# RWKV state step and decay product by heads: 64 rows and 64 columns each, in the two halves of a bank's partitions

## The reference

```python
def step(S, inp):
    r_t, w_t, k_t, v_t, a_t, b_t = inp
    sa = jnp.einsum('bhvk,bhk->bhv', S, a_t)
    S = S * w_t[:, :, None, :] + sa[..., None] * b_t[:, :, None, :] + v_t[..., None] * k_t[:, :, None, :]
    return S, jnp.einsum('bhvk,bhk->bhv', S, r_t)
```

## Time and profile before

| | us |
|---|---|
| median of 3 runs | 3189.41 |
| lowest, highest | 3189.28, 3194.16 |
| the profiled execution | 3187.53 |
| its span, first to last instruction | 3185.4 |
| TensorE busy, share of the span | 2967.0, 93% |
| VectorE busy | 2137.2, 67% |
| ScalarE busy | 1572.4, 49% |
| mean granted clock of TensorE | 0.975 |

### The profile page before, as it was taken

How to read it: one execution, slowest core, us unless ns; L and a number is a source line. 1 busy time by engine, 2 the same in 40 slices (tenths; PEclk the granted TensorE clock), 3 DMA queues, 4 the chain that set the end, 5 groups by cost and what they waited for, 6 DMA issues and landing times.

```text
span 3185.4 us, 50274 instructions
## 1 busy us (share of the span) xinstructions
PE 2967.0 (93%) x19942; PEld 2651.2 (83%) x19942; DVE 2137.2 (67%) x3465; ACT 1572.4 (49%) x2606; POOL 714.3 (22%) x885
## 2 busy tenths in 40 slices
PE   4876999999999997899999899888999999999998
PEld 4865998888888887788888788766788888888887
DVE  8787877765777557667766666555756665566655
ACT  3445555543555444455555555344544444344443
POOL 5356402210112000765555410000100111001100
PEclk9987999999999999999999999998999999999999
DMA  4411555556555555322222222422555555555554
GB/s 178 161 67 40 168 176 189 194 171 198 200 186 186 167 166 175 119 79 91 87 87 87 94 90 100 166 80 90 174 181 176 187 194 171 190 211 186 189 170 144
DMA packets 78953, 475.20 MB, mean 149 GB/s; under 512 B 8129, under 2 KB 11201, under 8 KB 37441
## 3 DMA queue, kind: packets, MB, share of 16 engines
q1 hardware_dynamic: 76480, 459.66, 42.5%
q10 hardware_dynamic: 2240, 12.32, 1.1%
HBM read 465.66 MB, written 6.29 MB: 148 GB/s over the span
## 4 chain that ended last, share of the span: by engine, by line
PE 75%; DVE 13%; ACT 7%; issue 2%; POOL 2%; DMA 0%; ACTq 0%; DVEq 0%; SPq 0%; POOLq 0%
PE bank L692 33%; PE bank L696 22%; PE bank L694 5%; PE bank L695 4%; DVE m L1185 3%; ACT m L2006 2%; PE bank L708 1%; DVE m L1839 1%; PE bank L994 1%; POOL m L2679 1%; POOL m L2675 1%; PE bank L995 1%; PE bank L1109 1%; PE bank L991 1%; PE bank L997 1%
## 5 line engine op out<-in xcount | busy, mean ns | idle before, releaser
L696 PE MATMUL bank<-m,m 128*128 128x256 f32 x6864 | 1932.0, 281 | 0.0
L692 PE MATMUL bank<-m,m 128*128 128x512 f32 x4736 | 1656.6, 394 | 2.5 <-ACT m L2497 2.0
L1185 DVE TENSOR_TENSOR m<-m,m 128x1024 fp32r<-128x1024 f32 (+1 forms) x944 | 1076.7, 1149 | 615.0 <-ACT m L2006 609.0
L696 PEld LDWEIGHTS bank<-m,m 128*128 128x128 f32 x6864 | 1302.5, 190 | 1.2
L2006 ACT ACTIVATE m<-m 128x1024 fp32r<-128x1024 f32 (+1 forms) x944 | 911.8, 979 | 724.0 <-PE bank L696 697.4
L692 PEld LDWEIGHTS bank<-m,m 128*128 128x128 f32 x4736 | 890.0, 188 | 200.8 <-issue 2.5
L694 PE MATMUL bank<-m,m 128*128 128x256 f32 x2128 | 643.4, 302 | 74.2 <-DVE m L1185 67.2
L695 PE MATMUL bank<-m,m 128*128 128x256 f32 x2128 | 607.7, 286 | 0.0
L694 PEld LDWEIGHTS bank<-m,m 128*128 128x128 f32 x2128 | 413.6, 194 | 104.5 <-issue 87.8
L695 PEld LDWEIGHTS bank<-m,m 128*128 128x128 f32 x2128 | 414.2, 195 | 3.6 <-issue 1.9
L2656 POOL TENSOR_TENSOR m<-m,m 128x256 fp32r<-128x256 f32 x44 | 63.4, 1441 | 695.6 <-ACT m L2228 695.6
(11 more groups left out here) (368 smaller groups left out, 3057.5 us busy)
## 6 DMA issues: line engine op xcount, KB each, us to landing
m<-in_w_up SPq DMA_DIRECT2D x88, 1024.0 KB, 4.8
m<-in_w_down SPq DMA_DIRECT2D x128, 704.0 KB, 4.0
m<-in_w_gu SPq DMA_DIRECT2D x88, 1024.0 KB, 4.9
m<-in_w_out SPq DMA_DIRECT2D x48, 1024.0 KB, 5.0
m<-in_w_krv SPq DMA_DIRECT2D x48, 1024.0 KB, 4.8
m<-in_w_xbc SPq DMA_DIRECT2D x24, 1024.0 KB, 4.9
m<-in_w_z SPq DMA_DIRECT2D x16, 1024.0 KB, 4.8
m<-in_w_in SPq DMA_DIRECT2D x14, 1024.0 KB, 4.9
```

The lines of the kernel that those rows point to most:

```text
L692: pe.matmul(bank.rearrange("p (a b) -> p a b", a=2), hi, x, start=kc == L.k0, stop=False)
L696: m = pe.matmul(ps, lo, x[:, 0, :], start=False, stop=last)
L1185: v.tensor_tensor(lo_of(k), raw_of(k)[0], hi_of(k).bitcast(F32), SUB).then_inc(*lo_v(("lo", k)))
```

## The change

The decay product becomes two: for each half R of the partitions, the 64 columns R of the weights with the 64 columns R of each of the four chunks (256 columns), written into the partitions R of the bank. Lines 994, 995 and 997 become two each: for each half R, 64 columns of weights with 64 columns, written into rows R and columns R of the bank. In line 997 the old state's columns R still enter with all 128 rows. Line 991, all waits, all signals and what VectorE and ScalarE do are as before; the signal of each group sits on its last matmul. The off-diagonal parts of the bank, which nothing reads, are not computed.

```diff
@@ -977,8 +977,10 @@
                 yield
                 pe.wait_ge(*wkv_a["bkx", i, hf])
                 pe.wait_ge(*wkv_v["q", i, hf])
-                pe.matmul(bB[:, :], wub[:, 128:256], bxb.rearrange("p c k -> p (c k)"), start=True,
-                          stop=True).then_inc(*wkv_pe(("g", i, hf)))
+                for R in HALVES:
+                    m = pe.matmul(bB[R, :].rearrange("p (c k) -> p c k", c=4)[:, :, R], wub[:, 128:256][:, R],
+                                  bxb[:, :, R], start=True, stop=True)
+                m.then_inc(*wkv_pe(("g", i, hf)))
                 yield
                 pe.wait_ge(*wkv_v["g", i, hf])
                 for c in range(4):
@@ -991,10 +993,13 @@
                         m = pe.matmul(bA[:, Q], sb_, qb[:, Q], start=False, stop=c == 3)
                         if c == 3:
                             m.then_inc(*wkv_pe(("y", i, hf)))
-                    pe.matmul(bB[:, 0:128], bxb[:, c, :], wub[:, 0:128], start=True, stop=False)
-                    m = pe.matmul(bB[:, 0:128], kxb[:, c, :], tk[:, TV, :], start=False, stop=first)
+                    for R in HALVES:
+                        pe.matmul(bB[R, R], bxb[:, c, R], wub[:, R], start=True, stop=False)
+                    for R in HALVES:
+                        m = pe.matmul(bB[R, R], kxb[:, c, R], tk[:, TV, R], start=False, stop=first)
                     if not first:
-                        m = pe.matmul(bB[:, 0:128], gb[:, c, :], sb_, start=False, stop=True)
+                        for R in HALVES:
+                            m = pe.matmul(bB[R, R], gb[:, c, R], sb_[:, R], start=False, stop=True)
                     m.then_inc(*wkv_pe(("s", i, hf, c)))
                     yield
```

## The result

| | before | after |
|---|---|---|
| median, us (12 runs each) | 3189.49 | 3183.85 |
| lowest, highest | 3188.92, 3194.16 | 3177.97, 3187.22 |
| profiled execution, us | 3187.53 | 3187.22 |
| its mean granted clock | 0.975 | 0.970 |

The ratio is 0.9979 (95% interval 0.9971 to 0.9988): 5.6 us faster by the medians, where 18 were forecast. The direction was right and the size was three times too large. The same kernel on another chip gave 3183.3 (11 runs, ratio 0.9977).

The account below looks back on a forecast made before the run. TensorE's own stream was taken as the bound in most rounds. State steps and decay products together shorten it by 22.7 us, of which four fifths, 18 us, get through: forecast 3171 us, range 3158 to 3186.

Parts of the forecast that it names:

- The price of a half-width pass: State step and decay product on TensorE: a pair of passes with 64 columns takes 0.055 us, bounds 0.04 and 0.11.
- the overlap of the halves: TensorE's half-width passes: the two halves run side by side, the second pair starting some 0.06 us behind the first.
- the 0.10 us of emptying: At each change of width TensorE empties for 0.10 us; in and out, with the bare loads, 0.365 us.
- the bare loads: Weight loads not hidden at a change of width: 0.055 us into half width, 0.11 us into full width.
- the counts of neighbours: Steps with line 991, by following work: 74 of 112 save 0.055 us each, 30 save 0.42, 8 save 0.265.
- program-order: Rival, 8%: second half waits for the first half's second pass; 8.9 us of stream left, 7 get through, 3182 us.
- no-overlap rivals: Rival, 5%: halves do not overlap at this size, each pair costs 0.11 us; 31 us slower, 3221 us.
- What gets through: Of 22.7 us saved in TensorE's stream, four fifths become time, 18 us; TensorE's waits swallow the rest.
- a rival with 7%: Clock falls, or unseen costs, 7%: clock 0.96 over some 560 us of the stage loses 22 us against 18 gained, 3193.
- The sign that I named for this rival: Trace after: a granted clock below 0.98 from 1400 to 1700 us would show the forecast wrong.
- VectorE takes over after 1760: Rival, 15%: all gain outside 1400 to 1760 us is swallowed, 13 us stay, 3177 us.
- Waits at line 991 grow: TensorE's waits at line 991, for the evacuation of the previous state, grow by some us.

Follow-up runs that it names:

- the second set: The changed kernel, not altered, run once more on another chip beside later runs: 3183.30 us, ratio 0.9977 to the kernel before.
- The full-width run with less work: Kernel before with the decay product streaming 256 of its 512 columns at full width, leaving out chunks 2 and 3: 3190.13 us, ratio 1.0001.
- the filler: Changed kernel plus five unused full-width fp32 products ahead of line 993's wait (line 991 before), even pairs 0 to 10: 3180.17 us; in the kernel before 3189.54.
- before with prep split: Kernel before with VectorE's last five operations of prep split over two rounds: 3192.37 us, ratio 1.0005.
- decay alone: Kernel before with only the decay product by heads, the state step at full width: 3191.98 us, ratio 1.0009.
- 256 columns: Kernel before with the decay product streaming 256 of its 512 columns at full width: 3190.13 us, ratio 1.0001.
- state alone: Changed kernel with the decay product back at full width, only the state step by heads: 3186.65 us, ratio 0.9995 to the kernel before.
- changed with prep split: Changed kernel with VectorE's last five operations of prep split over two rounds: 3182.67 us, ratio 0.9977 to the kernel before.
- line 991 by heads, decay at full width: Changed kernel with line 991 also by heads and the decay product back at full width: 3178.33 us, ratio 0.9962 to the kernel before.
- line 991 by heads: Changed kernel with line 991 also made two half-width products of 64 weight columns and 32 columns: 3171.75 us, ratio 0.9947 to the kernel before.
- the three with the filler: Five spare products in TensorE's wait: changed kernel 3180.17 us, kernel before 3189.54, changed kernel with line 991 also by heads 3173.33.

## Why the prediction was wrong

- **The price of a half-width pass, the overlap of the halves, the 0.10 us of emptying, the bare loads and the counts of neighbours**: right, each within 0.02 us a step, but for 16 of the decay products (0.13 for 0.08); sum 21.5 by kinds of rounds, 22.6 by the balance, for 22.7. The program-order and no-overlap rivals did not come: four passes in 0.11 us.
- **What gets through** is the step that failed. I let four fifths through, for waits alone, 4.5 us of loss, and put the clock's share at nothing. The waits took about what I gave them, 5.6 us in the blocks. The clock took 12.0 us there (14 by the mean clock of the 12 runs, 9 by the second set), and 5.0 us were left of 22.6.
- **The missing term is the clock.** I had it as a rival with 7% and made it hang on the emptied 0.10 us and on a loss over the whole stage. What I held against it, that a stretch with TensorE busy 137 of 145 us holds 1.00, says nothing of what follows a single wait. In its place the runs showed falls behind waits that the shorter stream lengthens: eight slow stretches in the blocks instead of two. Of the six further ones, four follow waits for VectorE (at 1379 behind 1.84 us, 1.66 before; at 1553 and 1706 behind 1.7, 1.35 before; at 1959 behind 1.21, 0.70 before) and two follow waits for ScalarE (at 1792 behind 1.94, 1.89 before; at 1884 behind 1.88, 1.66 before). The full-width run with less work shows that a shorter stream brings it without half width too, the filler that the wait does. Why the one fall comes and the other does not stays open. I read the waits and the clock of before in two separate views and never asked what stands ahead of a fall. The sign that I named for this rival, a clock below 0.98 from 1400 to 1700 us, did not come (0.99) although the clock was the cause: only one of the six further falls lies in that stretch.
- **VectorE takes over after 1760**: the place was wrong. The long waits for VectorE recur every 77 us from 1473 on, in the rounds with two preps; moving its work moved the wait.
- **Waits at line 991 grow**: right, from 14.7 to 18.3 us before that line by the groups of both traces. VectorE's and ScalarE's waits for line 997 shrank, as forecast, from 45.1 to 42.0 and from 53.5 to 40.6 us.
- The range, 3158 to 3186, held the time; the point did not.

## What to carry to other kernels

Two half-width products in the two halves of the partitions pay where the neighbours are half width as well: 12 of the 21.5 us of shorter stream were in 30 of 128 steps, and turning the last full-width product of the step into halves (line 991) brought more time, some 10 us, than the change as a whole. Before a shorter TensorE stream is booked as time, look at the waits that it lengthens and at what the granted clock does behind them; a test is to put spare products into the wait. Where VectorE's own work fills a round, the one rearrangement tried here moved the wait and did not shorten it.

## What the runs showed of the hardware

- A 64-column weight load with 64 streamed columns in both halves: a pair of passes each 0.055 us. The price of the 32-column passes, four of them, one in each quarter, in 0.04 us, was no guide to it.
- The granted clock fell to its lower level for 3.4 to 10.2 us at a time. All 68 slow stretches that begin between 1325 and 1985 us in the 13 profiles begin in a wait of TensorE or within 2.6 us behind the end of one. The wait that recurs four times between 1450 and 1710 us, two profiles of the changed kernel and one of each other version:

| versions | that wait, us | places with a fall behind it |
|---|---|---|
| before; before with prep split; decay alone; 256 columns | 1.3 to 1.4 | 0 of 16 |
| changed, on two chips; state alone; changed with prep split | 1.7 | 9 of 16 |
| line 991 by heads, decay at full width | 1.9 | 3 of 4 |
| line 991 by heads | 1.9 | 0 of 4 |
| the three with the filler | filled, at most 0.6 left | 0 of 12 |

What decides between places with the same wait stays open. The length alone is no rule: later in the stage a fall also followed waits of 1.2 us (at 1959 in the changed kernel).
- The changed kernel's executions differ by 9.3 us (3177.97 to 3187.22) where the kernel before differs by 5.2; the fastest of them has the clock of the kernel before, 0.975, and is 11.5 us faster than that kernel's median.
- Left open: the 3.6 us that the decay by heads alone costs, and why the further 11 us of shorter stream, with line 991 by heads, came at no further cost in clock.
